# One step more between the probabilities and their product with the values, and a ring of five slots for them

## The reference

```
h = einsum('bnd,de->bne', x, w_in)              # 1024 -> 3328 columns
qa, ka, va, ga, qb, kb, vb, gb = split(h)
out_a = dilated_attention(rope(qa), rope(ka), va) * silu(ga)
out_b = gqa_attention(axial_rope(rms(qb)), axial_rope(rms(kb)), vb) * silu(gb)
f = einsum('bne,ed->bnd', concat(out_a, out_b), w_out)
y = layer_norm(ALPHA * x + f)

# both attentions, for each head:
p = softmax(q @ k.T * scale + log(count))       # the dilated patterns become one mask
o = p @ v
```

## Time and profile before

| what | value |
| --- | --- |
| time, median of three runs | 470.45 us (470.15 to 471.06) |
| profiled execution, its own time | 469.93 us |
| span of the profile | 468.0 us |
| mean granted clock of PE | 0.966 of full speed |
| PE busy | 412.2 us (88%) |
| DVE busy | 301.8 us (64%) |
| ACT busy | 231.8 us (50%) |
| POOL busy | 224.1 us (48%) |

### The profile page before, as it was taken

One profiled execution on the slowest core, in us unless ns is written; L12 is line 12 of the kernel. 1 busy time (PEld: TensorE's weight loads), 2 busy tenths in 40 slices (PEclk: granted clock), 3 DMA queues, 4 the chain that ended last, 5 costly groups with the idle time before them and its releaser, 6 DMA issues.

```text
span 468.0 us, 6756 instructions
## 1 busy us (share of the span) xinstructions
PE 412.2 (88%) x2350; PEld 355.2 (76%) x2350; DVE 301.8 (64%) x713; ACT 231.8 (50%) x465; POOL 224.1 (48%) x230
## 2 busy tenths in 40 slices
PE   3999999487799989999999999999889669999980
PEld 2887988376688878889788888888778558788860
DVE  3622555723559778566768999977757445454997
ACT  5403220136456666666766566666755736321221
POOL 2821424361346547644644787747465675331221
PEclk9999999978999999999999999999998979999995
DMA  8821111120001101101110111031101116120113
GB/s 299 326 76 45 46 45 47 46 90 1 23 24 46 43 3 47 46 1 46 45 41 7 46 46 45 26 112 46 45 1 46 46 71 244 49 87 0 64 72 134
DMA packets 10112, 30.11 MB, mean 64 GB/s; under 512 B 1376, under 2 KB 1504, under 8 KB 10080
## 3 DMA queue, kind: packets, MB, share of 16 engines
q1 hardware_dynamic: 9936, 29.43, 17.8%
q10 hardware_dynamic: 144, 0.26, 0.2%
HBM read 26.54 MB, written 3.15 MB: 63 GB/s over the span
## 4 chain that ended last, share of the span: by engine, by line
PE 56%; DVE 21%; issue 10%; ACT 7%; POOL 5%; DMA 1%; DVEq 0%; ACTq 0%; POOLq 0%
PE bank L518 13%; PE bank L519 13%; PE bank L520 13%; PE bank L636 6%; PE bank L564 5%; DVE prob L991 3%; DVE p_lo L1005 2%; ACT prob L777 2%; PE bank L594 2%; PE bank L595 2%; DVE h L1127 2%; DVE k_st L971 2%; ACT w_hi L717 1%; DVE q_st L971 1%; POOL h L1174 1%
## 5 line engine op out<-in xcount | busy, mean ns | idle before, releaser
L1207 POOL TENSOR_SCALAR prob<-prob,den 128x512 f32<-128x512 f32 (+1 forms) x96 | 69.2, 726 | 74.8 <-DVE den L1000 74.8
L518 PE MATMUL bank<-t_hi,w_lo 128*128 128x512 f32 (+1 forms) x256 | 87.7, 343 | 2.0 <-DVE gate L1036 2.0
L520 PE MATMUL bank<-t_hi,w_hi 128*128 128x512 f32 (+1 forms) x256 | 86.6, 338 | 0.0
L519 PE MATMUL bank<-t_lo,w_hi 128*128 128x512 f32 (+1 forms) x256 | 86.4, 338 | 0.0
L786 ACT ACTIVATE p_hi<-bank 128x512 fp32r<-128x512 f32 x80 | 47.7, 597 | 74.0 <-PE bank L564 73.2
L1157 POOL TENSOR_TENSOR w_lo<-raw,w_hi 128x512 fp32r<-128x512 f32 x42 | 57.8, 1398 | 53.0 <-ACT w_hi L717 53.0
L1005 DVE TENSOR_TENSOR p_lo<-bank,p_hi 128x512 fp32r<-128x512 f32 x80 | 55.1, 689 | 42.4 <-ACT p_hi L786 41.6
L518 PE MATMUL bank<-w_hi,t_lo 128*128 128x512 f32 (+1 forms) x180 | 68.5, 380 | 15.0 <-DVE t_lo L898 8.1
L777 ACT ACTIVATE prob<-prob,nmax 128x512 f32<-128x512 f32 (+1 forms) x96 | 62.1, 647 | 34.0 <-DVE nmax L991 33.6
L519 PE MATMUL bank<-w_lo,t_hi 128*128 128x512 f32 (+1 forms) x180 | 67.2, 373 | 0.0
L520 PE MATMUL bank<-w_hi,t_hi 128*128 128x512 f32 (+1 forms) x180 | 66.8, 371 | 0.0
(11 more groups left out here) (136 smaller groups left out, 767.5 us busy)
## 6 DMA issues: line engine op xcount, KB each, us to landing
raw<-weights SPq DMA_DIRECT2D x31, 512.0 KB, 3.3
mix_t<-xt SPq DMA_DIRECT2D x8, 384.0 KB, 7.6
h<-x_prompt SPq DMA_DIRECT2D x4, 512.0 KB, 5.5
y_prompt<-h SPq DMA_DIRECT2D x8, 256.0 KB, 2.0
prob<-weights SPq DMA_DIRECT2D x2, 512.0 KB, 9.2
h<-x_sample SPq DMA_DIRECT2D x2, 512.0 KB, 8.8
y_sample<-h SPq DMA_DIRECT2D x4, 256.0 KB, 2.1
cst<-consts SPq DMA_DIRECT2D x1, 960.0 KB, 11.0
```

The costliest lines, as they stand in the source:

```text
L518: nc.tensor.matmul(out, a_lo, b_hi, start=first, stop=False)
L519: nc.tensor.matmul(out, a_hi, b_lo, start=False, stop=False)
L520: return nc.tensor.matmul(out, a_hi, b_hi, start=False, stop=last)
L1207: ins = nc.gpsimd.tensor_scalar(s, s, den[:, j % 2, t:t + 1], 0.5, ALU.mult, ALU.mult)
```

## The change

The product of a group comes in step v + 5 instead of v + 4 for a last unit v (`groups_at`), and the loop has one step more (STEPS is 85 instead of 84). PE's product, ACT's copy of the second part and DVE's sum move with it, and so do the gate products whose step follows from `groups_at`. The products then sit in steps 1, 3 and 4 modulo 5. The two pairs of slots become a ring of five slots, one for each unit of a head, used at unit modulo 5; a slot's next high part waits for the product of the group that held the unit five before. The memory grows from four to five times 512 columns for each of the two tiles. The weight units that reuse this memory in the end take the first four slots.

```
--- before.py
+++ after.py
@@ -55,7 +55,7 @@
 GROUPS = QT // 2 + 1
 PRING = 4
 LAG = 3
-STEPS = NU + LAG + 1
+STEPS = NU + LAG + 2
 NAT_ITEMS = 3 * TILES
 IN_ITEMS = NAT_ITEMS + 2 * NB
 
@@ -169,8 +169,8 @@
         q_st = sb("q_st", [P, 2, TOK], F32R)
         k_st = sb("k_st", [P, 2, 2, TOK], F32R)
         v_st = sb("v_st", [P, 2, TILES, 2 * HEAD_DIM], F32R)
-        p_hi = sb("p_hi", [P, 2, 2, SEQ], F32R)
-        p_lo = sb("p_lo", [P, 2, 2, SEQ], F32R)
+        p_hi = sb("p_hi", [P, UNITS, SEQ], F32R)
+        p_lo = sb("p_lo", [P, UNITS, SEQ], F32R)
         h = sb("h", [P, TILES, D_MODEL])
         hkv = sb("hkv", [P, TILES, 2 * KV_WIDTH])
         q_b = sb("q_b", [P, N_HEADS_B // 2, TOK])
@@ -268,7 +268,7 @@
             if n == 1:
                 return pieces(q_flat[:, 0:UW]), pieces(k_flat[:, 2 * UW:3 * UW])
             if n in (2, 3):
-                return [pieces(a[:, n - 2].rearrange("p a c -> p (a c)")) for a in (p_hi, p_lo)]
+                return [pieces(a[:, 2 * (n - 2):2 * (n - 1), :].rearrange("p a c -> p (a c)")) for a in (p_hi, p_lo)]
             return pieces(v_flat[:, 0:UW]), [v_flat[:, UW:UW + 512], q_flat[:, UW:UW + 512]]
 
         def weight(g, row, width, col=0, cols=None):
@@ -392,11 +392,8 @@
             return GROUPS * j + k // 2
 
         def groups_at(u):
-            v = u - LAG - 1
+            v = u - LAG - 2
             return [group_of(v)] if 0 <= v < NU and (v == NU - 1 or group_of(v + 1) != group_of(v)) else []
-
-        def transposed_at(u):
-            return group_of(u) % 2, u % UNITS % 2
 
         def mixed_through(j):
             return GROUPS * (j + 1)
@@ -625,10 +622,10 @@
                 o = o_ps[:, 0:2 * P].rearrange("p (t q) -> p t q", t=2)
                 for n in range(keys):
                     if sample:
-                        hi, lo = (a[:, g % 2, 0, :].rearrange("p (t n q) -> p t n q", n=ST, q=P)[:, :, n, :]
+                        hi, lo = (a[:, QT, :].rearrange("p (t n q) -> p t n q", n=ST, q=P)[:, :, n, :]
                                   for a in (p_hi, p_lo))
                     else:
-                        hi, lo = (a[:, g % 2, :, n * P:(n + 1) * P] for a in (p_hi, p_lo))
+                        hi, lo = (a[:, 2 * k:2 * k + 2, n * P:(n + 1) * P] for a in (p_hi, p_lo))
                     v = v_st[:, kv % 2, base + n, :]
                     passes = [(o, v, hi), (o[0:HEAD_DIM], v[:, 0:HEAD_DIM], lo)]
                     last = n == keys - 1
@@ -725,7 +722,7 @@
                 if n == 1:
                     return q_st[:].rearrange("p s t -> p (s t)")[:, 0:UW]
                 if n in (2, 3):
-                    return p_hi[:, n - 2].rearrange("p a c -> p (a c)")
+                    return p_hi[:, 2 * (n - 2):2 * (n - 1), :].rearrange("p a c -> p (a c)")
                 return v_st[:].rearrange("p s t d -> p (s t d)")[:, 0:UW]
 
             def x_high(k):
@@ -780,10 +777,9 @@
 
             def prob_high(u):
                 act.wait_ge(pt_ready, u + 1)
-                if group_of(u) >= 2:
-                    act.wait_ge(pv_done, group_of(u) - 1)
-                slot, at = transposed_at(u)
-                nc.scalar.activation(p_hi[:, slot, at, :], pt_ps[u % 2][:], ACT.Copy).then_inc(pt_hi_done, 1)
+                if u >= UNITS:
+                    act.wait_ge(pv_done, group_of(u - UNITS) + 1)
+                nc.scalar.activation(p_hi[:, u % UNITS, :], pt_ps[u % 2][:], ACT.Copy).then_inc(pt_hi_done, 1)
 
             def copy_low(g):
                 act.wait_ge(pv_done, g + 1)
@@ -1001,8 +997,8 @@
 
             def prob_low(u):
                 dve.wait_ge(pt_hi_done, u + 1)
-                slot, at = transposed_at(u)
-                nc.vector.tensor_tensor(p_lo[:, slot, at, :], pt_ps[u % 2][:], p_hi[:, slot, at, :].bitcast(F32),
+                slot = u % UNITS
+                nc.vector.tensor_tensor(p_lo[:, slot, :], pt_ps[u % 2][:], p_hi[:, slot, :].bitcast(F32),
                                         ALU.subtract).then_inc(pt_lo_done, 1)
 
             def mix(g):
```

## The result

| kernel | median (range) | runs | ratio to the kernel before, 95% interval |
| --- | --- | --- | --- |
| before | 470.3 us (469.12 to 471.06) | 4 | |
| changed | 464.82 us (462.68 to 465.24) | 4 | 0.9884 (0.9852 to 0.9915) |
| changed, run again (below) | 465.56 us (464.55 to 465.85) | 6 | 0.9896 (0.9874 to 0.9919) |

The change makes the kernel about 1.1% faster, some 5 us. That is the forecast sign and inside the range (464.0 to 472.5), but three times the 1.65 us of the sum. The profiled execution took 462.68 us, the fastest of its four; its span is 460.7 us.

The account below looks back on a forecast made before the run. PE, busy 88%, was taken as the bound, its idle time in the attention loop as winnable. +12.2 - 3.75 - 2.2 - 3.5 + 1.0 - 2.1 = 1.65 us gained, so 468.8 us forecast, range 464.0 to 472.5.

Parts of the forecast that it names:

- waits for the low part, 15 places: Products before step 71 lose 12.2 us waiting for DVE's low part; all of it was to go.
- sum, steps 9, 14, 19: Products there wait for DVE's sum of the product before, in the one output bank: 3.75 us lost together.
- sum, steps 24 to 39: Same wait for the sum where gates replace rotations: 0.5 to 0.6 us each, 2.2 us lost together.
- gaps that come back, less step 70: Losses returning as late sums where DVE binds, around steps 38, 44, 48, 68, less 0.5 from step 70's gate wait: -3.5 us.
- slide into POOL's wait: Around steps 72 to 77, the chain to POOL's split starts earlier, with step 72's product under it: 1.0 us gained.
- tail: Behind step 83's wait for POOL's weights, the last two products run later, the last waiting for a sum: 2.1 us lost.
- its bounds of 0.2 and 2.1: Late sum of step 48: 0.2 us if DVE's chain stays tied to the transposes, 2.1 if DVE runs unbroken; 2.1 taken.
- rival (d): Granted clock: new waits may bring a half-clock stretch, or step 70's shorter wait spare one; 1.7 us either way, no chance given.
- (a): Everything is kept: the sum is never late in the new pair, 11.1 us gained, 459.4 us; chance 0.08.
- (b): It cancels: sums and tail take back the low-part gain within 0.94 us, 470.4 us; chance 0.23.
- (c): Slower through the single output bank: gaps in steps 2 mod 5 return as late sums, 474.6 us; chance 0.18.
- The port term: DVE's multiplication in steps 8, 13, 18 stays at 1.57 us, not 0.76, while POOL's split shares the SBUF port: 2.4 us.

Follow-up runs that it names:

- second profile: Changed kernel executed again with nothing edited: 465.56 us; the kernel before was also profiled again, one execution of 471.37 us.
- Run 4: Changed kernel plus a second output bank, so products of odd groups use the bank of the early transposes: 456.95 us, ratio to before 0.9708.
- Run 2: Changed kernel with the ring of five slots kept but the product back in its old step v + 4: 469.51 us, ratio to before 1.0003.
- run 3: Kernel before with the product moved to step v + 5 but the two pairs of slots kept: 474.35 us, ratio 1.0093.
- run 7: Changed kernel with POOL's weight split queued behind its addition of the rotated halves: 463.13 us, ratio to before 0.9868.

## Why the prediction was right in sign and too small

| term of the sum | forecast | measured | from |
| --- | --- | --- | --- |
| waits for the low part, 15 places | +12.2 | +12.2 | none left in the list of waits (step 53's 0.7 was a wait for a sum) |
| sum, steps 9, 14, 19 | -3.75 | -3.65 | 1.18 + 1.29 + 1.18 |
| sum, steps 24 to 39 | -2.2 | -2.1 | 0.59 + 0.46 + 0.58 + 0.46 |
| gaps that come back, less step 70 | -3.5 | -2.4 | 0.5 - 0.54 - 1.24 - 1.11, below |
| waits for the gate in steps 25, 30, 35, 40 | none | +0.9 | 0.21 + 0.24 + 0.24 + 0.22, below |
| slide into POOL's wait | +1.0 | +0.9 | steps 72 and 73, same chain of 15.39 |
| tail | -2.1 | -2.0 | 4.22 instead of 2.19 from POOL's weights to the last product; 4.20 in the second profile |
| clock after step 70 | left out | +1.7 | 5 x 0.34, window of the earlier trace rows |

The measured terms add up to 5.5; the medians differ by 5.5 and 4.6 (465.56 against that run's 470.19). What remains is less than two executions of one kernel differ by.

**The mechanism held.** The low-part waits went entirely, the single bank made products of the close pair wait, and the first seven of these waits came within 0.15 us of their forecast. Run 4 shows that they were the price: with a second bank they vanish and the loop is 7.2 us shorter. Run 2 shows that the ring alone wins nothing, run 3 that the later product alone loses.

**The terms that were mis-sized.** Of the 3.9 us by which the sum fell short, 1.7 are the clock, below; 1.1 are "gaps that come back", -3.5 forecast, -2.4 measured; 0.9 are a wait that the prediction did not see. Of step 37's 1.66 us, 1.25 should have returned as a late sum behind step 38; the wait in step 39 is 0.46, as in step 29, so nothing returned. (That loss differs between executions: it is 1.2 us in the second profile of before and in that of run 2.) Step 49 lost 1.24, between its bounds of 0.2 and 2.1, of which the far end was taken. Steps 44 and 68 were given 0.6 and lost 0.54. Step 59 was given nothing and lost 1.11: there the sum itself stood 0.68 us waiting for ACT's copy, which stood behind exponentials that waited for DVE's mask, a detour for which the sum has no term:

```profile
303.56 0.72 ACT L774 ACTIVATE prob<-prob,nmax 128x512 f32<-128x512 f32 x1 [1.11 <-DVE nmax L987]
...
304.82 0.42 DVE L1008 TENSOR_TENSOR mix_t<-bank,o_lo 64x256 f32<-64x256 f32 x1 [0.68 <-ACT o_lo L789]
```

Step 70 came as forecast: the product of step 69, a sample's, lies wholly under the gate's wait, which shrinks from 2.01 to 1.55 us. From step 69's transposes to the awaited matmul it takes 4.51 us before (350.36 - 345.85) and after (342.83 - 338.32), the second time with the product in it, first a line of before, then of the changed kernel:

```profile
345.85 0.60 PE L564 MATMUL bank<-cst,prob 128*128 128x128 f32 x4
```

```profile
338.32 0.60 PE L561 MATMUL bank<-cst,prob 128*128 128x128 f32 x4
338.68 0.36 PE L633 MATMUL bank<-p_hi,v_st 128*128 128x256 f32 x1
...
342.83 0.47 PE L515 MATMUL bank<-t_hi,w_lo 128*128 128x512 f32 x1 [1.55 <-DVE gate L1032]
```

The wait that was not seen stands at the start of steps 25, 30, 35 and 40 of the kernel before, where a projection block follows a gate block, and is too short for the list of waits. From the transposes of step 24 to those of step 25:

```profile
192.33 0.60 PE L564 MATMUL bank<-cst,prob 128*128 128x128 f32 x4
...
192.54 0.69 DVE L1036 SCALAR_TENSOR_TENSOR gate<-gate,bank 128x512 f32<-128x512 f32 x1 [1.44 <-ACT gate L803]
...
193.00 0.40 PE L595 MATMUL bank<-k_st,q_st 128*128 128x512 f32 x1
...
193.37 0.47 PE L518 MATMUL bank<-t_hi,w_lo 128*128 128x512 f32 x1
...
194.83 0.60 PE L564 MATMUL bank<-cst,prob 128*128 128x128 f32 x4
```

The next block's first matmul starts 0.37 us after the last of the scores, behind the gate that ends at 193.23 and frees its bank. From transposes to transposes it takes 194.83 - 192.33 = 2.50 us, where it takes 2.29 from step 9 to step 10. In the changed kernel a product stands ahead of this matmul, and less the sum waits the two stretches are equally long (2.75 and 2.77 us). So of the 2.1 us of sum waits in steps 24, 29, 34 and 39 PE had lost 0.9 at the same places already.

**The clock** was named as rival (d), 1.7 us either way, and left out of the sum. The profiles bear out its sign: the stretch at 0.66 behind step 70's wait of 2.01 us stands in all three profiles in which products keep their old step (before twice, ring alone once), and in none of the eight in which that wait is 1.5 to 1.6 us. That the shorter wait is the cause is not shown: of the two profiles with a wait of 2.10 us one has the stretch and one has not, and step 67's 1.8 us brought it once in three. So it is a likelihood that the change lowers, not a fixed saving.

**The rivals.** (a), everything kept, is out at 459.4, because the sum was late as forecast. (b) and (c) are out: (c) needed 5.2 us of returning gaps, and 2.9 came. The median misses the interval of 466 to 469.5 that the prediction held for likeliest; that it lies inside the range, 0.8 us above its lower end, is owed to the range's width, which holds the clock's 1.7 us and the near bound of step 48. The port term was weighed rightly: with POOL out of the way (run 7) the multiplication takes 0.69 instead of 1.57, and the prediction's choice of 1.57 for the three waits gave 3.75 against 3.65 measured. The rule of the Trainium skill (SBUF — State Buffer, section "SBUF: two separate sides"), by which the waits stay as long as the two coincide, agrees with both.

## What to carry to other kernels

Moving a consumer one step later removes the wait for its input only if everything that it shares has slack of a step too: list its output bank and its input slots, and compare for each the new distance between neighbours with the time from one's start to the release. When a wait turns up in such a shared buffer, try a second buffer before a reordering of queues: here the bank won 7.2 us in the loop, and the reordering 0.6 (2.3 if its slow stretch is left out), or 3.8 where it was kept to the first forty steps, because each reordered queue delayed another engine's work. Before a gain is believed, take the stages in which nothing was changed out of the comparison: here 2.8 of the 7.3 us between the first two profiles lay ahead of the first moved instruction and were chance.

## What the runs showed of the hardware

Where DVE's large multiplication and POOL's split of a weight unit run together, in these traces the one that starts second waits until the first one's instruction ends. In the changed kernel's step 8 POOL starts 0.27 us ahead, and DVE takes 1.57 us instead of 0.69: it ends at 140.28, 0.56 after POOL's first subtraction, which ends at 139.72; POOL's second one, from 139.68 on, then takes 1.73 where the first took 1.28.

In the kernel with two banks, step 18, DVE starts 0.01 us ahead and takes 0.69. POOL's two operations are long in either case, 3.09 us here and 2.97 there, instead of the 2.5 to 2.7 that they take where no such multiplication runs (2.54 in step 23 of before, 2.73 in run 7):

```profile
172.71 0.69 DVE L1036 TENSOR_TENSOR turn<-turn,cst 128x512 f32<-128x512 f32 x1
172.72 3.09 POOL L1165 TENSOR_TENSOR w_lo<-raw,w_hi 128x512 fp32r<-128x512 f32 x2 [1.75 <-ACT w_hi L726]
```

A stretch at half clock before the loop, worth 1.7 us, comes and goes between executions of one kernel, and so do those behind waits of 2 us. It stands behind a wait of 2.66 us (PE's scores for DVE's copies of queries) that all thirteen profiles have, and eleven have the stretch. The kernel before took from 465.28 to 471.73 us in the executions on record, so a difference of about 2 us between two single ones says nothing.

Not tried: the other half of the one output bank as a second place for products. PE would write in it while DVE reads the first half, and the Trainium skill (PSUM — Partial Sum Buffer, section "PSUM bank collisions raise a hardware error") says that two engines may not be in one bank and quadrant at once. No run here shows it.
